# Layer 2 of a mixture-of-experts trunk: the experts' order made behind expert 0, one more expert with a fixed place, and another order of the last expert's work

## The chip, the cores and the metric

One Trainium2 chip, one of its cores. The metric is the device time of one execution in microseconds (us), lower is better. Beside it stands one profiled execution, whose span runs from its first to its last instruction. TensorE (PE in the profile) makes the matrix products; VectorE (DVE), ScalarE (ACT) and GpSimd (POOL) work beside it; SyncE (SP) issues the loads from the chip's memory (HBM).

## The reference, cut to what matters

Two layers on 256 tokens of width 1024. Each has a token mixer (pooling in layer 1, attention in layer 2) and then a mixture of 32 experts, each with a gate, an up and a down matrix of 1024 x 256, 1024 x 256 and 256 x 1024 floats. All arithmetic is float32.

```python
def hier_moe(h, w_group, w_expert, w_gate, w_up, w_down):
    g_prob = jax.nn.softmax((t @ w_group).astype(jnp.float32), axis=-1)
    g_w, g_sel = lax.top_k(g_prob, 1)
    ...
    e_val, e_sel = lax.top_k(e_logits, EXPERT_TOPK)          # top 2 of the 8 in the group
    ...
    for e in range(N_EXPERTS):
        he = jax.nn.silu(t @ w_gate[e]) * (t @ w_up[e])
        y = y + combine[:, e, None] * (he @ w_down[e])
```

Every expert's 3 MB of weights has to come from HBM; an expert sees only the few tokens that chose it.

## The kernel before

**The ring.** Weights come into a ring of four slots, each with room for the gate and up matrices (one load of 2 MB) and the down matrix (one load of 1 MB) of an expert. In what follows GU31 is the load of the gate and up matrices of the expert at place 31, and D31 that of its down matrix. SyncE issues all loads, in program order (the loop at L670): GU(p+1), then D(p), then GU(p+2), D(p+1) and so on to GU31, D30, D31, and last the 0.5 MB of the final norm's gains. A load waits for its slot: GU for `ring_free`, which ScalarE counts up when the gate and up products of the slot's last user are done (L1769), D for `down_free`, counted up after the down product (L1778).

**Places.** In layer 2 the experts 0 to `STAT` - 1 = 6 stand at places of their own number. Experts 4, 5 and 6 have room outside the ring and are loaded early. The other 25 are put in an order that depends on the routing: twelve experts with at most 16 tokens in each half ("light") first, in six pairs (`LIGHTS`), then the rest. The order comes about in three steps. VectorE computes a diagonal matrix (`order_experts`, L2259). TensorE multiplies it by ones (`order_rows`, L1056), which spreads the order over all partitions, in `order_at` of bank 1. VectorE turns that into integers and into lanes for the later compares (`places_by_rows`, L2278), and counts `off_ready` up to 3 and 4, on which SyncE (L667) waits before it reads which expert stands at place 7, and GpSimd before it copies tokens for places from 7 on.

**Units.** `UNITS` (L31) has 26 units, of one place or one light pair, numbered from 0: places 0, 1, 2, 3, the pair (7, 8), place 4, the pair (9, 10), 5, (11, 12), 6, three more pairs, and places 19 to 31. Units 24 and 25 are places 30 and 31. What one unit takes:

- *hidden*: the gate and up products on TensorE (into bank 0 or 1), then a silu on ScalarE and a multiplication on VectorE (`gate_he`);
- *turn*: `turn_he_of`, TensorE transposes the result, VectorE copies it back (`take_heT`);
- *down*: the down product into bank 2 or 3, which VectorE scales into `ye` (`take_ye`);
- *rows*: `rows_unit` adds `ye` to the tokens' rows in banks 4 to 7, by a matrix `share` that VectorE makes (`match_unit`, `share_unit`).

`expert_unit` (L1222) runs on TensorE, for unit u: turn of u-1, hidden of u, down of u-1, and where u is odd rows of u-3 and of u-2. In the last unit (25) it is turn of 24, hidden of 25, down of 24, turn of 25, rows of 22. Then `later_experts` (L1267) runs the down product of unit 25 in two halves of 256 columns, with rows of 23 between them and rows of 24 behind, and `last_rows` adds the last rows half by half. The final norm follows: squares on ScalarE (L2039), the gains, four stores.

**Around expert 0.** On TensorE the gather of the tokens (into hS, part of reg_a in the trace) stands first, then `order_rows`, then the hidden of expert 0 (`first_hidden`, L1066), then `table_light` twice, then turn and hidden of expert 1 (`second_hidden`). GpSimd copies each expert's tokens into xh before its hidden.

Of the kernel before, what the change touches and what calls it, by code (L numbers as in the profile page):

```python
# [7 lines left out]
P = 128  # L8
SEQ, D, F, E = 256, 1024, 256, 32
NG, EPG, TOPK = 4, 8, 2  # L10
NH, DH = 16, 64
T = SEQ // P
# [4 lines left out]
PAD = NSLOT + CAP  # L17
LIGHT = CAP // T
NLP = 6
STAT = 7  # L20
NQ = P // CAP
RANKS = 128
FAR = 65536.0
# [4 lines left out]
FRONT = R + 2  # L28
LOOPED = FRONT + (E - FRONT) // R * R
LIGHTS = [(STAT + 2 * n, STAT + 2 * n + 1) for n in range(NLP)]  # L30
UNITS = [(0,), (1,), (2,), (3,), LIGHTS[0], (4,), LIGHTS[1], (5,), LIGHTS[2], (6,)] + LIGHTS[3:] \  # L31
    + [(p,) for p in range(STAT + 2 * NLP, E)]
NU = len(UNITS)
COUNTED = (E, NU)
# [138 lines left out]
def program(nc, x, c, ada_w, ada_b, norm_mix_g, norm_ffn_g, pool_w, pool_scale, w_qkv, w_o,  # L173
# [3 lines left out]
    with ctx:  # L177
# [50 lines left out]
        pair_first, pair_step = in_alibi(NLP), in_alibi(NLP)  # L228
        light_lanes = in_alibi(T * NLP).rearrange("p (t n) -> p t n", t=T)
        order_f = in_alibi(E)  # L230
        ones = sb("ones", [P, P])
        qkb = sb("qkb", [P, 4])
        ccol = sb("ccol", [P, KC])
# [88 lines left out]
        chosen = ye[0:E, 1, 2 * P:2 * P + E]  # L322
        of_place = ye[0:E, 1, 2 * P + E:2 * P + 4 * E].rearrange("p (f n) -> p f n", f=3)
        order_diag = ye[0:E, 1, 2 * P + 4 * E:2 * P + 7 * E].rearrange("p (f n) -> p f n", f=3)
        of_place_sum = ye[0:E, 1, 2 * P + 7 * E:2 * P + 7 * E + 3]
# [167 lines left out]
        def _(sp):  # L493
# [170 lines left out]
            gate_up(1, 3, *exp_at(1, 3))  # L664
            sp.wait_ge(S("gf_full"), 2)
            up_part(1, early, R)
            sp.wait_ge(S("off_ready"), 3)  # L667
            e = expert_of(STAT)
            gate_up(1, e, *exp_at(1, STAT))
            for p in range(STAT, E):  # L670
                if p + 1 < E:
                    following = expert_of(p + 1)
                    gate_up(1, following, *exp_at(1, p + 1))
                down_part(1, e, *exp_at(1, p))
                e = following
                if p == STAT + 1:
# [156 lines left out]
        def _(pe):  # L833
# [222 lines left out]
            def order_rows():  # L1056

                pe.wait_ge(S("diag_ready"), T + 1)
                pe.wait_ge(S("hS_dve"), 2 * len(BY_DVE))
                mm(order_at, ones[0:E, :], order_diag, True, True).then_inc(S("counts"), 1)  # L1060

            def table_light(t):

# [2 lines left out]
            def first_hidden(L):  # L1066

                s, fill = loaded(L, 0)
                gu = gate_up_w(s).rearrange("p (g k j f) -> p k j g f", g=2, k=KC, j=2)
                pe.wait_ge(S("ring_first", s), fill)  # L1070
                pe.wait_ge(S("ring_mid", s), fill)
                for k in range(KC):
                    pe.wait_ge(S("xe_ready", L), 2 + k // 4)
                    for j in range(2):
                        last = mm(bank[0][j * 64:(j + 1) * 64, 0:F], xe[:, 0, k, :], gu[:, k, j, :, :], k == 0, k == KC - 1)
                last.then_inc(S("gu_ready", L), 1)
                if L == 0:
# [144 lines left out]
            def expert_unit(u):  # L1222

                b = u % 2
                turn_he_of(1, u - 1, 1 - b)
                hidden_unit(u, b)
                down_unit(u - 1, 1 - b, u >= 3)
                if u == NU - 1:
                    turn_he_of(1, u, 1)
                    rows_unit(u - 3, 0)  # L1230
                elif b:
                    rows_unit(u - 3, 0)
                    rows_unit(u - 2, 1)

            def last_rows(L):

# [30 lines left out]
            def later_experts(L):  # L1267

                n = COUNTED[L]
                if L == 0:  # L1270
                    experts(L, FRONT, LOOPED)
                    for e in range(LOOPED, E):
                        expert_at(L, e)
                else:
                    for u in range(2, NU):
                        expert_unit(u)
                n_ovf = beyond(pe, L)
# [367 lines left out]
            mixed_logits(4, 8)  # L1645
            route(1)
            gather(1)
            order_rows()
            for e in range(2):
                expert_at(1, e)  # L1650
            later_experts(1)
# [3 lines left out]
        def _(act):  # L1655
# [411 lines left out]
        def _(dve):  # L2067
# [94 lines left out]
            def route(L):  # L2162
# [82 lines left out]
                if L == 0:  # L2245
                    nc.vector.memset(hS[:, :, NSLOT:PAD], 0.0).then_inc(S("hS_pad"), 1)
                    take_gathered(L)
                else:
                    places_by_rows()

            def take_gathered(L):

# [6 lines left out]
            def order_experts():  # L2259
# [10 lines left out]
                then(nc.vector.tensor_scalar(chosen, place_of[0:E, :], own_part[0:E, :], None, ALU.is_equal))  # L2270
                tt(of_place[:, 0, :], chosen, of_expert[0:E, :], ALU.mult)
                then(tt(of_place[:, 1:3, :], offc[0:E, :].rearrange("p (t n) -> p t n", t=T),
                        chosen.unsqueeze(1).broadcast_to([E, T, E]), ALU.mult))
                then(nc.vector.tensor_reduce(of_place_sum, of_place, AX, ALU.add))
                tt(order_diag, ident[0:E, 0:E].unsqueeze(1).broadcast_to([E, 3, E]),
                   of_place_sum.unsqueeze(2).broadcast_to([E, 3, E]), ALU.mult).then_inc(S("diag_ready"), 1)

            def places_by_rows():  # L2278

                dve.wait_ge(S("counts"), 3)  # L2280
                then(nc.vector.tensor_scalar(order_f[0:1, :], order_at[0:1, 0:E], 1.0 / RANKS, None, ALU.mult))
                nc.vector.tensor_copy(order_i[:, :], order_f[0:1, :]).then_inc(S("off_ready"), 1)
                nc.vector.tensor_copy(off_at, order_at[0:1, E:3 * E]).then_inc(S("off_ready"), 1)
                nc.vector.tensor_scalar(lanes, order_at[:, 0:E], of_lane[:, 0:1], None, ALU.add)
                pairs = order_at[:, STAT:STAT + 2 * NLP].rearrange("p (n x) -> p x n", x=2)
                then(nc.vector.tensor_copy(pair_first, pairs[:, 0, :]))
                then(tt(pair_step, pairs[:, 1, :], pair_first, ALU.subtract))
                then(stt(pair_first, pair_step, second, pair_first, ALU.mult, ALU.add))
# [97 lines left out]
            def expert_unit(u):  # L2386

                b = u % 2
                if u:
                    take_heT(1, u - 1, 1 - b)  # L2390
                if u == 1:
                    dve.wait_ge(S("tab_ready"), 2)
                    for g in range(4):
                        rows = slice(32 * g, 32 * g + 32)
# [10 lines left out]
                    share_unit(u - 2, b)  # L2405
                gate_he(1, u, b)
                if u == 0:
                    count_beyond(1)
                if u >= 2 and b == 0:
                    if u > 2:  # L2410
                        dve.wait_ge(S("rows_added", 1), u - 2)
                    take_ye(1, u - 1, 1)

            def expert(L, e, b, ahead_rows=False, next_rows=False):

# [73 lines left out]
            def later_experts(L):  # L2489
# [3 lines left out]
                    for e in range(LOOPED, E):  # L2493
                        expert_at(L, e)
                else:
                    for u in range(NU):
                        expert_unit(u)
                n_ovf = beyond(dve, L)
                take_heT(L, n - 1, 1)
                if L:  # L2500
                    match_unit(n - 2)
                    dve.wait_ge(S("rows_added", L), n - 3)
                take_ye(L, n - 2, 0)
                if L:
                    share_unit(n - 2, 0)
# [248 lines left out]
```

## Time and profile before

| | us |
|---|---|
| median of the runs | 690.08 |
| lowest, highest of 3 runs | 689.83, 690.11 |
| the profiled execution, its own time | 690.19 |
| span of the profiled execution | 688.5 |
| TensorE busy in it | 626.9 (91%) |
| VectorE, ScalarE, GpSimd busy | 251.1, 120.1, 60.5 |
| moved by DMA | 273.32 MB, mean 397 GB/s |

The profile's page gives the busy time of each engine, the span in 40 slices with the clock that TensorE was granted, the moved bytes for each slice, the chain of work that ended last, and the costliest groups of instructions. The trace behind it gives the single instructions with what ended the idle time before them. A float32 product shows as two matmul records with a weight load each.

### The profile page before, as it was taken

The numbers are of one execution on the slowest core, as the hardware profiler recorded it, in microseconds if no ns is written. First come the engines' busy times: TensorE is split into PE (matmuls) and PEld (weight loads), VectorE is DVE, ScalarE is ACT, GpSimd is POOL, SyncE is SP. The second block draws the span as 40 slices with busy tenths as digits, with TensorE's granted clock in tenths as the row PEclk, the third lists the DMA queues.
The fourth block names the chain that finished last, engine by engine and source line by source line (L and its number), as shares of the span: only waits on it lengthen the run. The fifth ranks groups of instructions, "written<-read, shape, count | busy, mean of one in ns | idle before, by whom it ended". The sixth has DMA issues, their size and how long they took to land.

```text
span 688.5 us, 12940 instructions
## 1 busy us (share of the span) xinstructions
PE 626.9 (91%) x4790; PEld 383.7 (56%) x4790; DVE 251.1 (36%) x668; ACT 120.1 (17%) x312; POOL 60.5 (9%) x187
## 2 busy tenths in 40 slices
PE   4889899999899999999999999999999867998885
PEld 1445465554455555556888788886544324454452
DVE  1014433222222223245689495247332302222223
ACT  4013530000000000014244333237100000000003
POOL 7000021101001001100000000001111100001000
PEclk9999999999999999999999999999999979999998
DMA  9999999999999999999997989963999999999992
GB/s 354 417 420 422 428 421 433 430 428 431 433 430 428 430 428 426 423 420 421 418 422 282 413 343 426 422 277 127 390 425 420 427 427 421 425 426 423 425 419 97
DMA packets 27259, 273.32 MB, mean 397 GB/s; under 512 B 3141, under 2 KB 3653, under 8 KB 4937
## 3 DMA queue, kind: packets, MB, share of 16 engines
q1 hardware_dynamic: 27208, 272.65, 94.7%
q8 instruction: 32, 0.52, 0.3%
q14 instruction: 19, 0.15, 0.1%
HBM read 271.59 MB, written 1.05 MB: 396 GB/s over the span
## 4 chain that ended last, share of the span: by engine, by line
PE 80%; DMA 11%; issue 5%; ACT 1%; DVE 1%; SPq 1%; ACTq 0%; POOL 0%; DVEq 0%
PE bank L835 71%; DMA ring<-in_ada_w_dram 9%; PE bank L1043 6%; DMA ring<-in_exp_w_dram 2%; PE bank L1218 1%; PE bank L1526 1%; SPq L510 0%; ACT hx L2039 0%; PE bank L1380 0%; PE bank L1387 0%; DVE ye L2080 0%; ACT reg_b L1845 0%; ACT reg_a L1710 0%; ACTq L177 0%; DVE ye L2077 0%
## 5 line engine op out<-in xcount | busy, mean ns | idle before, releaser
L835 PE MATMUL bank<-ring,xh 128*64 128x256 f32 (+2 forms) x2496 | 306.0, 429 | 34.9 <-issue 33.9
L835 PEld LDWEIGHTS bank<-ring,xh 128*64 128x64 f32 (+1 forms) x2496 | 169.6, 134 | 132.2 <-issue 75.9
L2077 DVE TENSOR_TENSOR reg_c<-reg_c,bank 128x128 f32<-128x128 f32 x58 | 16.7, 288 | 183.0 <-ACT reg_c L1733 96.5
L763 POOL COPY xh<-reg_a 128x256 f32 (+1 forms) x106 | 41.2, 399 | 410.9 <-PE bank L835 287.2
L835 PE MATMUL bank<-reg_b,ring 128*128 128x256 f32 x256 | 57.2, 380 | 0.4 <-ACT reg_b L1890 0.4
L1043 PE MATMUL bank<-ye,reg_b 32*128 32x512 f32 (+1 forms) x432 | 52.8, 599 | 0.0
L835 PEld LDWEIGHTS bank<-reg_b,ring 128*128 128x128 f32 x256 | 48.0, 190 | 7.1 <-issue 0.9
L2077 DVE TENSOR_TENSOR ye<-bank,reg_c 128x512 f32<-128x512 f32 (+1 forms) x60 | 40.2, 670 | 29.5 <-PE bank L835 29.0
L2341 DVE COPY xh<-bank 128x128 f32<-128x128 f32 x58 | 16.6, 285 | 93.0 <-PE bank L835 93.0
L835 PE MATMUL bank<-ring,cact 128*32 128x512 f32 (+1 forms) x320 | 34.0, 535 | 16.5 <-DMA ring<-in_ada_w_dram 16.4
L1733 ACT ACTIVATE reg_c<-bank 128x128 f32<-128x128 f32 x32 | 8.9, 277 | 203.9 <-PE bank L835 203.9
L1770 ACT ACTIVATE reg_c<-bank 128x128 f32<-128x128 f32 x26 | 7.2, 277 | 185.0 <-PE bank L835 185.0
L835 PEld LDWEIGHTS bank<-cst,reg_c 128*64 128x64 f32 (+1 forms) x240 | 15.4, 138 | 39.5 <-issue 38.3
L1043 PEld LDWEIGHTS bank<-ye,reg_b 32*128 32x128 f32 x432 | 19.3, 184 | 31.1 <-issue 31.0
L835 PE MATMUL bank<-reg_a,ring 128*128 128x256 f32 x160 | 35.8, 381 | 0.0
L2080 DVE SCALAR_TENSOR_TENSOR ring<-ring,cact 128x1024 f32<-128x1024 f32 x28 | 34.2, 1279 | 0.3 <-DVE ring L2080 0.3
L835 PEld LDWEIGHTS bank<-reg_a,ring 128*128 128x128 f32 x160 | 30.0, 190 | 5.5 <-ACT reg_a L1657 0.8
L835 PE MATMUL bank<-ring,reg_b 128*128 128x256 f32 x128 | 28.9, 383 | 0.0
L835 PEld LDWEIGHTS bank<-ring,cact 128*32 128x32 f32 x320 | 8.1, 110 | 34.6 <-DMA ring<-in_ada_w_dram 17.3
L835 PEld LDWEIGHTS bank<-ring,reg_b 128*128 128x128 f32 x128 | 23.9, 190 | 4.1 <-issue 1.1
L835 PE MATMUL bank<-cst,reg_c 128*64 128x128 f32 (+1 forms) x240 | 25.3, 285 | 0.6 <-DVE reg_c L2165 0.6
L2080 DVE SCALAR_TENSOR_TENSOR reg_b<-reg_b,cst 128x256 f32<-128x256 f32 x52 | 24.8, 477 | 0.3 <-issue 0.2
(212 smaller groups left out, 457.0 us busy)
## 6 DMA issues: line engine op xcount, KB each, us to landing
ring<-in_exp_w_dram SPq DMA_DIRECT2D x41, 2048.0 KB, 20.3
ring<-in_exp_w_dram SPq DMA_DIRECT2D x20, 3072.0 KB, 16.0
ring<-in_ada_w_dram SPq DMA_DIRECT2D x48, 1024.0 KB, 17.7
ring<-in_exp_w_dram SPq DMA_DIRECT2D x44, 1024.0 KB, 21.0
ring<-in_w_qkv_dram SPq DMA_DIRECT2D x12, 1024.0 KB, 16.3
ring<-in_w_o_dram SPq DMA_DIRECT2D x4, 1024.0 KB, 8.4
gu_spare<-in_exp_w_dram SPq DMA_DIRECT2D x1, 2048.0 KB, 20.3
hx<-in_exp_w_dram SPq DMA_DIRECT2D x2, 1024.0 KB, 19.5
```

The source lines that it names most:

```text
L763: nc.gpsimd.tensor_copy(xe[:, b, k0:k1, t * CAP:(t + 1) * CAP], hS[:, k0:k1, bass.ds(off, CAP)])\
L835: return nc.tensor.matmul(o_, l_, r_, start=start, stop=stop)
L1043: yield nc.tensor.matmul(bank[4 + half + 2 * t][:, c0:c1], share[rows, b, :], ye[rows, b, c0:c1], start=False, stop=stop, skip_group_check ...
L1218: last = nc.tensor.matmul(bank[4 + half + 2 * t][:, :], share_light[rows, b, t, :], ye[rows, b, :], start=False, stop=False, skip_group_ch ...
L1526: last = nc.tensor.transpose(bank[5 + a][:, s * P:(s + 1) * P], sc[m % 2][a][:, s * P:(s + 1) * P], ident)
L1733: nc.scalar.activation(sil[:, b, :], bank[b][:, 0:P], ACT.Silu).then_inc(S("sil_ready", L), 1)
L1770: nc.scalar.activation(sil[:, u % 2, :], bank[u % 2][:, 0:P], ACT.Silu).then_inc(S("sil_ready", 1), 1)
L2077: return nc.vector.tensor_tensor(o_, a_, b_, op)
L2080: return nc.vector.scalar_tensor_tensor(o_, a_, s_, b_, op0, op1)
L2341: nc.vector.tensor_copy(heT[:, b, :], bank[b][:, 2 * P:3 * P]).then_inc(S("heT_ready", L), 1)
```

## The change

Three things are changed.

1. `STAT` goes from 7 to 8. Expert 7 has a fixed place and is a unit of its own, at index 4; the pairs begin at place 8, and 20 to 31 are single. There are still 26 units, and units 24 and 25 are still places 30 and 31. SyncE issues GU7 ahead of its wait for the order; the loop from there on issues the same loads in the same sequence.
2. The order's product on TensorE stands behind the hidden of expert 0, ahead of `table_light`, over 128 partitions where it had 32. VectorE copies `order_at` out (`keep_order`) behind `gate_he` of unit 0, and TensorE waits for that copy (`counts_read` 3) before the hidden of expert 1, which writes to the same bank. `places_by_rows` works from the copy, in unit 1 ahead of the table's copies, and `count_beyond` moves from unit 0 to unit 1.
3. The last unit has a function of its own on TensorE and on VectorE; ScalarE waits for the down product of unit 24 ahead of the silu of unit 25.

```diff
-STAT = 7
+STAT = 8
-UNITS = [(0,), (1,), (2,), (3,), LIGHTS[0], (4,), LIGHTS[1], (5,), LIGHTS[2], (6,)] + LIGHTS[3:] \
+UNITS = [(0,), (1,), (2,), (3,), (7,), LIGHTS[0], (4,), LIGHTS[1], (5,), LIGHTS[2], (6,)] + LIGHTS[3:] \
...
+            e = STAT - 1
+            gate_up(1, e, *exp_at(1, e))
             sp.wait_ge(S("off_ready"), 3)
-            e = expert_of(STAT)
-            gate_up(1, e, *exp_at(1, STAT))
-            for p in range(STAT, E):
+            for p in range(STAT - 1, E):
...
                 pe.wait_ge(S("diag_ready"), T + 1)
-                pe.wait_ge(S("hS_dve"), 2 * len(BY_DVE))
-                mm(order_at, ones[0:E, :], order_diag, True, True).then_inc(S("counts"), 1)
+                mm(order_at, ones[:, :], order_diag, True, True).then_inc(S("counts"), 1)
...
+                    order_rows()
                     pe.wait_ge(S("diag_ready"), 2 * T + 1)
                     table_light(0)
...
+                if L:
+                    pe.wait_ge(S("counts_read"), 3)
...
+            def last_unit():
+
+                u = NU - 1
+                turn_he_of(1, u - 1, 0)
+                rows_unit(u - 3, 0)
+                down_unit(u - 1, 0, True)
+                hidden_unit(u, 1)
+                rows_unit(u - 2, 1)
+                turn_he_of(1, u, 1)
+                rows_unit(u - 1, 0)
...
                 down(bank[3], down_w(s), 1, 0, 256).then_inc(S("dn_ready", L), 1)
-                if L:
-                    add_rows_of(L, n - 3, 1)
                 down(bank[1], down_w(s), 1, 256, 512).then_inc(S("dn_ready", L), 1)
-                add_rows_of(L, n - 2, 0)
+                if L == 0:
+                    add_rows_of(L, n - 2, 0)
...
+                if u == NU - 1:
+                    act.wait_ge(S("dn_ready", 1), u)
                 act.wait_ge(S("gu_ready", 1), u + 1)
...
+            def keep_order():
+
+                dve.wait_ge(S("counts"), 3)
+                nc.vector.tensor_copy(order_kept, order_at).then_inc(S("counts_read"), 1)
+                dve.wait_ge(S("counts_read"), 3)
```

On TensorE around expert 0, before: the 128x96 product from ye is the order's, the 64x256 ones into bank 0 are the hidden of expert 0, those into bank 1 the hidden of expert 1, the 128x512 ones the two tables.

```order
L835 MATMUL bank3<-keep,reg_b 128x256 x2
L835 MATMUL bank1<-ye,ones 128x96
L835 MATMUL bank0<-ring,xh 64x256 x16
L835 MATMUL bank2<-keep,ones 128x512
L835 MATMUL bank3<-keep,ones 128x512
L835 MATMUL bank0<-cst,reg_c 64x128 x2
L835 MATMUL bank1<-ring,xh 64x256 x16
```

And after, the same place:

```order
L836 MATMUL bank3<-keep,reg_b 128x256 x2
L836 MATMUL bank0<-ring,xh 64x256 x16
L836 MATMUL bank1<-ye,ones 128x96
L836 MATMUL bank2<-keep,ones 128x512
L836 MATMUL bank3<-keep,ones 128x512
L836 MATMUL bank0<-cst,reg_c 64x128 x2
L836 MATMUL bank1<-ring,xh 64x256 x16
```

The order's product went past the sixteen products of expert 0; nothing else moved here.

On TensorE at the end, before: cst,reg_c is a turn, 64x256 x16 a hidden, 64x512 x4 a down, 64x256 x4 half of the last down, ye,reg_b 128x512 x4 the rows of one unit. It begins with the turn of unit 24.

```order
L835 MATMUL bank<-cst,reg_c 64x128 x2
L835 MATMUL bank<-ring,xh 64x256 x16
L835 MATMUL bank<-ring,xh 64x512 x4
L835 MATMUL bank<-cst,reg_c 64x128 x2
L1043 MATMUL bank<-ye,reg_b 128x512 x4
L437 TENSOR_LOAD ov_n
L437 ISA x2
L835 MATMUL bank<-ring,xh 64x256 x4
L1043 MATMUL bank<-ye,reg_b 128x512 x4
L835 MATMUL bank<-ring,xh 64x256 x4
L1043 MATMUL bank<-ye,reg_b 128x512 x4
```

After, from the same turn on:

```order
L836 MATMUL bank<-cst,reg_c 64x128 x2
L1044 MATMUL bank<-ye,reg_b 128x512 x4
L836 MATMUL bank<-ring,xh 64x512 x4
L836 MATMUL bank<-ring,xh 64x256 x16
L1044 MATMUL bank<-ye,reg_b 128x512 x4
L836 MATMUL bank<-cst,reg_c 64x128 x2
L1044 MATMUL bank<-ye,reg_b 128x512 x4
L438 TENSOR_LOAD ov_n
L438 ISA x2
L836 MATMUL bank<-ring,xh 64x256 x8
```

Rows of 22 and the down of 24 went ahead of the hidden of 25; rows of 23 and of 24 stand behind it, and the two halves of the last down follow one another with nothing between.

## Rows read from the trace of the kernel before

**Rows 1.** The page: memory traffic in 40 equal slices of the span.
```profile
GB/s 354 417 420 422 428 421 433 430 428 431 433 430 428 430 428 426 423 420 421 418 422 282 413 343 426 422 277 127 390 425 420 427 427 421 425 426 423 425 419 97
```

**Rows 2.** Waits of the load queue: for whom, us in total, times, longest.
```profile
SPq L590 <- DVE off_i L2283: 10.9, 1, 10.9
```

**Rows 3.** Timeline, 475.8 to 482.3: start, us, engine, line, operation, count, idle before.
```profile
475.90 0.43 PE L835 MATMUL bank<-ye,ones 32*128 32x96 f32 x2 [0.16 <-DVE reg_a L2256]
476.00 0.51 POOL L763 COPY xh<-reg_a 128x128 f32 x1 [1.90 <-ACT reg_a L1710]
476.65 3.67 PE L835 MATMUL bank<-ring,xh 128*64 128x256 f32 x32 [0.32 <-POOL xh L763]
...
477.27 0.20 DVE L2283 CAST off_i<-bank 1x64 int32<-1x64 f32 x1
...
480.26 1.98 PE L835 MATMUL bank<-keep,ones 128*128 128x512 f32 x4
480.45 0.28 ACT L1770 ACTIVATE reg_c<-bank 128x128 f32<-128x128 f32 x1 [2.09 <-PE bank L835]
```

**Rows 4.** TensorE's timeline in the routing: two small products with ones, 128x64 each.
```profile
466.54 0.65 PE L835 MATMUL bank<-ye,ones 128*128 128x64 f32 x4
```

**Rows 5.** Timeline of the load queue, 478 to 495: GU7 and GU8 (one row), D7.
```profile
480.62 6.09 SPq L549 DMA_DIRECT2D ring<-in_exp_w_dram  x2
488.01 0.33 SPq L555 DMA_DIRECT2D ring<-in_exp_w_dram  x1
```

**Rows 6.** Two stretches: from:to, us, TensorE busy, its clock, DMA share, GB/s.
```profile
484.00:486.00 2.00, 2.00 (x22) 1.00 1.02 434
486.00:488.00 2.00, 2.00 (x16) 1.00 0.95 320
```

**Rows 7.** DMA issues, median us to landing: GU7 (480.62), GU8 (486.37), GU20 (580.30).
```profile
ring<-in_exp_w_dram SPq DMA_DIRECT2D x1, 2048.0 KB, 7.6
ring<-in_exp_w_dram SPq DMA_DIRECT2D x1, 2048.0 KB, 8.5
ring<-in_exp_w_dram SPq DMA_DIRECT2D x1, 2048.0 KB, 13.4
```

**Rows 8.** Timeline of the load queue, 640 to 655: GU31; D30 and D31.
```profile
643.56 0.34 SPq L549 DMA_DIRECT2D ring<-in_exp_w_dram  x1
645.20 7.81 SPq L555 DMA_DIRECT2D ring<-in_exp_w_dram  x2
```

**Rows 9.** DMA issues, us to landing: GU31 (issued 643.56), then D30 (issued 645.20).
```profile
ring<-in_exp_w_dram SPq DMA_DIRECT2D x1, 2048.0 KB, 25.4
ring<-in_exp_w_dram SPq DMA_DIRECT2D x1, 1024.0 KB, 26.3
```

**Rows 10.** Timeline of all engines, 666.9 to 681.2.
```profile
667.04 0.39 PE L835 MATMUL bank<-cst,reg_c 128*64 128x128 f32 x4
...
669.10 5.39 PE L835 MATMUL bank<-ring,xh 128*64 128x256 f32 x40 [1.67 <-issue]
672.89 0.28 ACT L1770 ACTIVATE reg_c<-bank 128x128 f32<-128x128 f32 x1 [6.99 <-PE bank L835]
...
674.29 0.42 PE L835 MATMUL bank<-cst,reg_c 128*64 128x128 f32 x4
...
674.64 1.14 PE L1043 MATMUL bank<-ye,reg_b 32*128 32x512 f32 x8
...
675.71 1.08 PE L835 MATMUL bank<-ring,xh 128*64 128x256 f32 x8
...
677.79 1.08 PE L835 MATMUL bank<-ring,xh 128*64 128x256 f32 x8
...
678.81 2.00 PE L1043 MATMUL bank<-ye,reg_b 32*128 32x512 f32 x24
678.92 0.42 DVE L2077 TENSOR_TENSOR ye<-bank,reg_c 128x256 f32<-128x256 f32 x1 [0.37 <-PE bank L835]
680.83 0.60 ACT L2039 ACTIVATE hx<-bank 128x512 f32<-128x512 f32 x1 [6.14 <-PE bank L1043]
```

**Rows 11.** Stretches around two idle times of TensorE; columns as in rows 6.
```profile
549.00:557.00 8.00, 0.00 (x0) 0.67 1.02 428
570.00:572.00 2.00, 0.15 (x4) 1.00 0.98 410
572.00:574.00 2.00, 2.00 (x24) 0.56 1.07 455
```

**Rows 12.** TensorE's timeline, 570 to 579: hidden and down of one unit.
```profile
571.85 7.06 PE L835 MATMUL bank<-ring,xh 128*32 128x256 f32 x80 [3.63 <-issue]
```

More of the change, by code:

```diff
@@ L230, in program @@
         order_f = in_alibi(E)
+        order_kept = in_alibi(3 * E)
         ones = sb("ones", [P, P])
@@ L321, in program @@
         spread = ye[:, 1, 2 * P:4 * P].rearrange("p (v q) -> p v q", v=2)
[L322 to L325, printed above, removed]
+        chosen = ye[:, 1, 2 * P:2 * P + E]
+        of_place = ye[:, 1, 2 * P + E:2 * P + 4 * E].rearrange("p (f n) -> p f n", f=3)
+        order_diag = ye[:, 1, 2 * P + 4 * E:2 * P + 7 * E].rearrange("p (f n) -> p f n", f=3)
+        of_place_sum = ye[:, 1, 2 * P + 7 * E:2 * P + 7 * E + 3]
         Ssb = xe[:, 0, :, :].rearrange("p k c -> p (k c)")[:, 0:SEQ]
@@ L675, in _ @@
                 e = following
-                if p == STAT + 1:
+                if p == STAT:
                     sp.wait_ge(S("tab_full"), 2)
@@ L1227, in expert_unit @@
                 down_unit(u - 1, 1 - b, u >= 3)
[L1228 to L1231, printed above, removed]
+                if b:
                     rows_unit(u - 3, 0)
                     rows_unit(u - 2, 1)
+            def last_unit():
[7 more added lines that the diff above has]
+                rows_unit(u - 1, 0)
             def last_rows(L):
@@ L1274, in later_experts @@
                 else:
-                    for u in range(2, NU):
+                    for u in range(2, NU - 1):
                         expert_unit(u)
+                    last_unit()
                 n_ovf = beyond(pe, L)
@@ L1647, in _ @@
             gather(1)
-            order_rows()
             for e in range(2):
@@ L2247, in route @@
                     take_gathered(L)
-                else:
-                    places_by_rows()
             def take_gathered(L):
@@ L2269, in order_experts @@
                 then(tt(place_of[:, free], others, moved, ALU.add))
[L2270 to L2273, printed above, removed]
+                then(nc.vector.tensor_scalar(chosen, place_of, own_part, None, ALU.is_equal))
@@ L2274, in order_experts @@
+                tt(of_place[:, 0, :], chosen, of_expert, ALU.mult)
+                then(tt(of_place[:, 1:3, :], offc.rearrange("p (t n) -> p t n", t=T),
+                        chosen.unsqueeze(1).broadcast_to([P, T, E]), ALU.mult))
                 then(nc.vector.tensor_reduce(of_place_sum, of_place, AX, ALU.add))
-                tt(order_diag, ident[0:E, 0:E].unsqueeze(1).broadcast_to([E, 3, E]),
-                   of_place_sum.unsqueeze(2).broadcast_to([E, 3, E]), ALU.mult).then_inc(S("diag_ready"), 1)
+                tt(order_diag, ident[:, 0:E].unsqueeze(1).broadcast_to([P, 3, E]),
+                   of_place_sum.unsqueeze(2).broadcast_to([P, 3, E]), ALU.mult).then_inc(S("diag_ready"), 1)
@@ L2278, in places_by_rows @@
+            def keep_order():
+                dve.wait_ge(S("counts"), 3)
+                nc.vector.tensor_copy(order_kept, order_at).then_inc(S("counts_read"), 1)
+                dve.wait_ge(S("counts_read"), 3)
             def places_by_rows():
-                dve.wait_ge(S("counts"), 3)
-                then(nc.vector.tensor_scalar(order_f[0:1, :], order_at[0:1, 0:E], 1.0 / RANKS, None, ALU.mult))
+                then(nc.vector.tensor_scalar(order_f[0:1, :], order_kept[0:1, 0:E], 1.0 / RANKS, None, ALU.mult))
@@ L2282, in places_by_rows @@
                 nc.vector.tensor_copy(order_i[:, :], order_f[0:1, :]).then_inc(S("off_ready"), 1)
[L2283 to L2287, printed above, removed]
@@ L2288, in places_by_rows @@
-                then(stt(pair_first, pair_step, second, pair_first, ALU.mult, ALU.add))
+                nc.vector.tensor_copy(off_at, order_kept[0:1, E:3 * E]).then_inc(S("off_ready"), 1)
+                nc.vector.tensor_scalar(lanes, order_kept[:, 0:E], of_lane[:, 0:1], None, ALU.add)
+                pairs = order_kept[:, STAT:STAT + 2 * NLP].rearrange("p (n x) -> p x n", x=2)
+                then(tt(pair_step, pairs[:, 1, :], pairs[:, 0, :], ALU.subtract))
+                then(stt(pair_first, pair_step, second, pairs[:, 0, :], ALU.mult, ALU.add))
@@ L2391, in expert_unit @@
                 if u == 1:
+                    places_by_rows()
                     dve.wait_ge(S("tab_ready"), 2)
@@ L2407, in expert_unit @@
                 if u == 0:
+                    keep_order()
+                if u == 1:
                     count_beyond(1)
@@ L2412, in expert_unit, with last_unit @@
                     take_ye(1, u - 1, 1)
+            def last_unit():
+                u = NU - 1
+                take_heT(1, u - 1, 0)
+                match_unit(u - 2)
+                dve.wait_ge(S("rows_added", 1), u - 3)
+                share_unit(u - 2, 1)
+                match_unit(u - 1)
+                dve.wait_ge(S("rows_added", 1), u - 2)
+                share_unit(u - 1, 0)
+                take_ye(1, u - 1, 0)
+                gate_he(1, u, 1)
             def expert(L, e, b, ahead_rows=False, next_rows=False):
@@ L2495, in later_experts @@
                 else:
-                    for u in range(NU):
+                    for u in range(NU - 1):
                         expert_unit(u)
+                    last_unit()
                 n_ovf = beyond(dve, L)
                 take_heT(L, n - 1, 1)
[L2500 to L2505, printed above, removed]
+                if L == 0:
+                    take_ye(L, n - 2, 0)
+                else:
                     match_unit(n - 1)
```

## The prediction

> **What bounds the kernel now.** I read the page first, then the waits and the timeline of the load queue, then the trace at the two places that the change touches. The traffic by slices [rows 1] is the view to begin with: nearly every slice stands at 420 to 430 GB/s, so the kernel is a stream of weights. The exceptions are slices in the middle (277 and 127 GB/s at 448 to 482 us), where the stream stops, and the last slice. From 484 us on the stream is full to near its end [rows 6]. So the time is made of three parts: when the stream of layer 2's experts starts again, its bytes at some 425 GB/s, which the change leaves alone, and what still has to be done when the last pieces have landed. TensorE is busy for 91% of the span, but in the last third it waits for each second gate and up load; a product moved there counts only if it lies behind the last landing.
>
> Where the stream starts again: SyncE waits for the order [rows 2], and the conversion that ends this wait runs from 477.27 for 0.20 us [rows 3]. GU7 is nevertheless issued only at 480.62 [rows 5], 0.17 us after the silu of expert 0 begins at 480.45 [rows 3]. That silu marks the end of expert 0's gate and up products, which frees slot 0. So the slot comes last, by some 3 us, and not the order.
>
> **The fixed place of expert 7.** GU7 no longer waits for the order, but it still waits for slot 0. Gain: 0. The order is now needed for GU8, whose slot 1 comes free with expert 1's hidden; before, GU8 was issued at 480.62 + 6.09 - 0.33 = 486.38 [rows 5]. The order now comes at: he of unit 0, turn, its copy on VectorE (about 483.3), then two short steps of VectorE, about 483.8, and some 0.6 us of SyncE to read it. That is 2 us ahead of the slot, so nothing. With 26 units still, and one single unit earlier, TensorE's sum of work over the units is the same. In the middle the stream is held by free slots, and its reserve is thinnest where GU20 landed 13.4 us after its issue, against 7.6 for a load of its size into an empty queue [rows 7]: 5.8 us of reserve, and a shift of the pairs by one unit moves the issue times by less. Nothing.
>
> **The order's product.** Before, it ran 475.90 to 476.33, while GpSimd still copied expert 0's tokens (476.00 to 476.51); expert 0 began at 476.65, released by that copy [rows 3]. It lay in idle time and cost nothing, so taking it away from there gives nothing (at the very most the 0.32 us that TensorE waited). Behind expert 0 TensorE has no idle time: the tables start at once, at 480.26 [rows 3]. There it costs its full length: at most the 0.43 us that its row shows, with a drain that now lies beside other work, and about as much as one of two similar products that took 0.65 together, 0.33 each [rows 4]. I take 0.25, between nothing and 0.43. The wait for the copy of the order adds nothing: VectorE is done with he of unit 0 by 481.2 and with a copy of 96 columns by 481.5, when TensorE is still in the tables (to 482.2). What is queued behind this wait on TensorE is expert 1's hidden, and behind it GU8. So GU8 is issued 0.25 later. Does this reach the stream? GU8 was already late: in 486 to 488 the traffic fell to 320 GB/s, from 434 [rows 6], and GU8 took 8.5 us to land, 0.9 more than into an empty queue [rows 7]. So the stream had all but run dry when GU8 came, and a delay goes through nearly in full: 0.2 us, between 0 and 0.43. On VectorE the steps of `places_by_rows` and of the count (8 and 8 small instructions, most of about 0.2 us like the one at 477.27 [rows 3]) now lie in unit 1; queued behind them is the copy of unit 1's turn, which TensorE needs only after the hidden of unit 2, 5 us later, and the load of D6 waits for the count, but stands behind D8. Nothing.
>
> **The last unit.** This is the term that decides. The new order puts the down product of unit 24, which needs D30, ahead of the hidden of unit 25, which needs GU31. GU31 is issued before D30 [rows 8] and landed at 643.56 + 25.4 = 668.96; D30 landed at 645.20 + 26.3 = 671.50 [rows 8, 9]. Before, TensorE began the hidden at 669.10, 0.14 after GU31 landed, after an idle time of 1.67 us [rows 10]. Now:
>
> - turn of 24 to 667.43, rows of 22 in the idle time, to about 668.45;
> - down of 24 not before 671.50 + 0.14 = 671.64. Its length: hidden and down take 669.10 to 674.29 = 5.19, the hidden of it to the silu at 672.89, 3.75, so the down takes 1.44 [rows 10];
> - hidden of 25 from 673.08, where it was 669.10: 3.98 later, to 676.83.
>
> What is saved behind it: before, from the end of the hidden at 672.85 to the first square on ScalarE at 680.83 there were 7.98 us [rows 10]. Now there are rows of 23, 1.07 (674.64 to 675.71, which also covers silu and he); the turn, 0.35 (674.29 to 674.64); rows of 24, 1.07; two halves of the last down, 2 x 1.02 (677.79 to 678.81); and from there a wait that was covered by rows of 24: the second half of ye starts 0.11 after the down's end and takes 0.42 [rows 10], with the passing on some 0.65, then the last four rows. From the start of rows of 24 at 678.81 to the square took 2.02; that row holds 24 records in 2.00 us, of which rows of 24 are the wide half, 0.97, and the first half of the last rows a quarter, 0.48; less these it leaves 0.57. The sum is 1.07 + 0.35 + 1.07 + 2.04 + 0.65 + 0.57 = 5.75, so 2.23 saved. Net 3.98 - 2.23 = 1.75 us later. The last down, wanted from 679.3, finds D31 there: it is queued right behind D30 (issued at 645.20 + 7.81 - 0.33 = 652.7 [rows 8]), and 1 MB at 425 GB/s is 2.5 us, so it lands at about 674. The final norm behind it is as before. ScalarE's new wait for the down of 24 ends at 673.1, before the silu it stands ahead of; it delays nothing.
>
> **Sum.** 690.19 (the profiled execution, span 688.5 and 1.69 around it) + 0.20 + 1.75 = 692.14. That execution is 0.11 above the median of the runs, so the prediction for the median is **692.0**. With the bounds (front 0 to 0.43 and at best -0.32; the tail +-0.4 for the lengths of pieces taken from single rows) it is 691.2 to 692.7.
>
> **Rivals.**
>
> *The clock falls in the new idle time.* TensorE would stand still from 668.45 to 671.64, 3.2 us. In this trace idle times of 1.67 us leave the clock at its full level, 2.4 GHz; an idle time of 8 us took it to half of that (the mean in the stretch is 0.67), and after one of 3.63 us [rows 12], with 0.15 us of work in the 2 us at its end, the clock stood at a mean of 0.56 [rows 11], nearer to the 1.2 GHz level. Hidden and down then took 578.85 - 571.85 = 7.0 us at least, against 5.2. If this happens in the tail it costs 1.7 us more: 693.7. For it: 3.2 is near 3.63. Against it: the turn and the rows stand right ahead of it. What the Trainium skill says, in "TensorE: Matmul & The Clock Gate", Part 1 on the clock gate, is that the array falls to 1.2 GHz after it has been idle and comes back only after sustained work; the trace agrees at 572 us, and by that rule the cost is the same 1.7. Chance 0.15.
>
> *D30 is there in time, and the tail gains.* If D30 were landed with GU31, the down of 24 would start at 669.10, the hidden at 670.54, 1.44 later, and with 2.23 saved the end would come 0.79 earlier: 690.08 + 0.20 - 0.79 = 689.5, not slower. The point from which it decides: D30 no more than 0.8 us behind GU31; at 671.50 against 668.96 it is 2.54 behind, about what 1 MB takes at 425 GB/s (2.5). Both come by one queue, D30 second. The Trainium skill ("DMA: Bandwidth & Descriptors", Queues, rings and completion order) has it that each DMA engine takes its descriptors in the order of the ring; the landings agree, and this speaks against the rival. Since loads come in pieces on 16 engines, and I may misjudge which wait stands where, 0.12.
>
> *The front gains.* If the first products of expert 0 were held by the order's product after all, the stream would start up to 0.32 earlier, and the sum is 691.4. Chance 0.06. *The order was what held GU7*: it would then go out at 477.5, and the stream would start 3 us earlier, some 689; the slot's release stands against it. Chance 0.03.
>
> *The stream runs dry in the middle.* TensorE's idle times move by a unit, and with the clock halved behind them a slot could come free late by more than the 5.8 us of reserve; a us or two, 693. Chance 0.04.
>
> **How the numbers follow.** The forecast as worked out has 0.60. What a measurement of this kernel can tell from no change is 0.2%, 1.4 us, so the line to "slower" runs at 691.5. The forecast's own lower edge (691.2) and the front's gain lie just under it and give "within" about 0.07 beside the 0.12 of the early D30; faster by over 0.2% has 0.04, nearly all from the order that held GU7. Slower has the rest, 0.77. The range for 8 in 10 runs from 690.9, below the forecast's edge and the front's gain, to 693.8, with the clock's fall; left out are the early D30, the GU7 case and what would lie above.
>
> **What would show it.** In the profile after: the order's product right behind expert 0, expert 0 still at about 476.6, and GU7 issued at about 480.6; GU8 at about 486.6; full traffic from there; rows of 22 right behind the turn of 24, then TensorE idle for about 3.2 us until D30 lands near 671.7, the hidden of 25 from about 673.3, the first square near 682.8. The prediction is wrong if the idle time ahead of the down of 24 is under 1.5 us, if GU7 is issued well before 480, or if the tail's pieces lie apart by more than their lengths.

## The result

| | before | after |
|---|---|---|
| median of the runs, us | 690.10 | 693.92 |
| lowest, highest of 4 runs | 689.83, 690.52 | 693.76, 694.92 |
| span of the profiled execution | 688.5 | 692.3 |

The changed kernel is slower: the ratio of its runs to those of before is 1.0058, with a 95% interval of 1.0046 to 1.007. That is 3.8 us, where 1.9 were forecast, and 0.1 us above the range.

**The front.** The first view is the timeline of the changed kernel around expert 0 (start, us, engine, line, operation); it answers to [rows 3].

```profile
476.09 0.51 POOL L764 COPY xh<-reg_a 128x128 f32 x1 [1.89 <-ACT reg_a L1720]
476.74 3.67 PE L836 MATMUL bank<-ring,xh 128*64 128x256 f32 x32 [0.91 <-POOL xh L764]
...
480.34 0.46 PE L836 MATMUL bank<-ye,ones 128*128 128x96 f32 x2
480.54 0.28 ACT L1782 ACTIVATE reg_c<-bank 128x128 f32<-128x128 f32 x1 [2.08 <-PE bank L836]
...
480.64 1.91 PE L836 MATMUL bank<-keep,ones 128*128 128x512 f32 x4
```

Expert 0 begins at 476.74, released by GpSimd's copy as before (476.65); the place that the order's product left is now idle time, 0.91 in place of 0.32. Behind expert 0 the product costs 0.30 us: the tables begin at 480.64, 0.30 behind the product's start. The load queue, as in [rows 5]:

```profile
480.55 6.47 SPq L550 DMA_DIRECT2D ring<-in_exp_w_dram  x2
488.18 0.38 SPq L556 DMA_DIRECT2D ring<-in_exp_w_dram  x1
```

GU7 goes out with the slot, at 480.55 (before 480.62), and GU8 at 480.55 + 6.47 - 0.33 = 486.69, 0.31 later than before. Of this 0.09 is the start of expert 0 itself, which lies between 476.47 and 476.96 in the profiled executions of all kernels here. Counted from that start, GU8 goes out after 9.95 us where it was 9.73, so 0.22 later.

**The tail.** The load queue of the changed kernel at the end, and how long GU31 (issued 643.82) and D30 (issued 645.46) took to land, answering to [rows 8, 9]:

```profile
643.82 0.34 SPq L550 DMA_DIRECT2D ring<-in_exp_w_dram  x1
645.46 7.81 SPq L556 DMA_DIRECT2D ring<-in_exp_w_dram  x2
```

```profile
ring<-in_exp_w_dram SPq DMA_DIRECT2D x1, 2048.0 KB, 25.4
ring<-in_exp_w_dram SPq DMA_DIRECT2D x1, 1024.0 KB, 26.3
```

So GU31 landed at 669.22 and D30 at 671.76, both 0.26 later than before. And the timeline of the end, against [rows 10]:

```profile
667.30 0.39 PE L836 MATMUL bank<-cst,reg_c 128*64 128x128 f32 x4
...
667.62 1.14 PE L1044 MATMUL bank<-ye,reg_b 32*128 32x512 f32 x8
...
671.83 7.08 PE L836 MATMUL bank<-ring,xh 128*64 128x512 f32 x40 [3.06 <-DMA ring<-in_exp_w_dram]
...
678.84 1.14 PE L1044 MATMUL bank<-ye,reg_b 32*128 32x512 f32 x8
679.02 0.28 ACT L1782 ACTIVATE reg_c<-bank 128x128 f32<-128x128 f32 x1 [12.86 <-PE bank L836]
...
684.62 0.60 ACT L2051 ACTIVATE hx<-bank 128x512 f32<-128x512 f32 x1 [3.81 <-PE bank L1044]
```

Behind the rows of unit 22 TensorE stands still for 3.06 us, until D30 lands. The row that follows is the down product of unit 24 and the hidden of unit 25 in one. Before, the same 40 records took 5.19 us to the next instruction; here they take 678.84 - 671.83 = 7.01. The stretches of the changed kernel tell why (from:to, us, TensorE busy, its granted clock, DMA share, GB/s):

```profile
668.00:670.00 2.00, 0.76 (x8) 1.00 0.99 412
670.00:672.00 2.00, 0.17 (x2) 1.00 0.92 379
672.00:674.00 2.00, 2.00 (x8) 0.70 0.47 188
674.00:676.00 2.00, 2.00 (x10) 0.50 0.06 25
676.00:678.00 2.00, 2.00 (x20) 0.95 0.00 0
```

After the idle time the clock falls from 2.4 to 1.2 GHz (0.50 in 674 to 676) and is back at about 676. The first square comes at 684.62, 3.79 later than before. That is the whole difference of the spans (692.3 - 688.5).

The account of these 3.79 us, from the start of the hidden at 669.10 before: the down product starts at 671.83, 2.73 later (0.26 of this is the stream, which came later); it takes 1.44 itself at full clock; the two products together take 7.01 - 5.19 = 1.82 longer, most of it by the halved clock (1.69 and 0.13 for the new order itself, as experiments 3 and 5 show); behind it 684.62 - 678.84 = 5.78 are left, where 7.98 were, 2.20 saved. 2.73 + 1.44 + 1.82 - 2.20 = 3.79.

### The profile page after: what moved, and what is told of

It reads as the page before. It is cut to its first block, busy times and chain, and to the rows that moved or that the text cites. A ratio compares the mean times of both kernels' runs of the same rounds, so it can differ in the third digit from the quotient of the medians.

```text
span 692.3 us, 12936 instructions
## 1 busy us (share of the span) xinstructions
PE 632.3 (91%) x4790; PEld 385.0 (56%) x4790; DVE 251.1 (36%) x668; ACT 120.1 (17%) x312; POOL 60.5 (9%) x187
## 4 chain that ended last, share of the span: by engine, by line
PE 80%; DMA 13%; issue 4%; DVE 1%; ACT 1%; SPq 1%; ACTq 0%; POOL 0%; DVEq 0%
PE bank L836 71%; DMA ring<-in_ada_w_dram 9%; PE bank L1044 6%; DMA ring<-in_exp_w_dram 4%; PE bank L1221 2%; PE bank L1537 1%; SPq L511 0%; ACT hx L2051 0%; PE bank L1391 0%; PE bank L1398 0%; DVE ye L2092 0%; ACT reg_b L1857 0%; DVE ye L2089 0%; ACT reg_a L1720 0%; ACTq L177 0%
## 5 line engine op out<-in xcount | busy, mean ns | idle before, releaser
L836 PE MATMUL bank<-ring,xh 128*64 128x256 f32 (+3 forms) x2496 | 308.3, 432 | 35.3 <-issue 30.5
```

The costliest lines, as they stand in the source:

```text
L836: return nc.tensor.matmul(o_, l_, r_, start=start, stop=stop)
```

## The experiments

The theory to test: the new last unit holds nearly all of the loss, by the wait for D30 and by the clock that this wait costs; the front is a matter of 0.2 to 0.3 us. Rivals: the stream suffers in the middle; the new order of the tail is slow by itself; the excess over the forecast has another cause than the clock. All times are medians, beside runs of the kernel before on the same chip; a comparison with the changed kernel is one with its 693.92 us.

### 1. The front of the change alone

The changed kernel with `last_unit` taken out again on TensorE and VectorE, and ScalarE's wait with it.

```diff
-                    for u in range(2, NU - 1):
+                    for u in range(2, NU):
                         expert_unit(u)
-                    last_unit()
...
```

> The front of the change alone (expert 7 at a fixed place, the order's product behind expert 0), with the last unit as before. Theory A (the new last unit holds nearly all of the loss; the front only puts 0.2 to 0.3 us of TensorE work ahead of expert 1): 690.3 to 690.4 us against 690.1, the two last loads landing 0.2 to 0.3 later. Rival B (the stream of loads suffers in the middle from the shifted pairs): 691 or more, with slices under 400 GB/s between 500 and 660 us.

Measured: 690.38 us against 690.20, ratio 1.0002 (0.9993 to 1.0011): no difference that can be told. In its profile the hidden of unit 25 starts at 669.38, 0.28 later than before:

```profile
669.38 5.39 PE L836 MATMUL bank<-ring,xh 128*64 128x256 f32 x40 [1.69 <-issue]
```

Its slices of memory traffic from 500 to 650 us stand at 420 to 428 GB/s. The rival with a stream that suffers in the middle falls.

### 2. The new last unit alone

The kernel before, with `last_unit`, the closing lines of `later_experts` and ScalarE's wait as in the change.

> The new last unit alone, on the front of before. Theory A: 693.6 us, that is 3.5 to 3.6 over before, of which about 1.75 is the wait of the down product of unit 24 for its load D30 and about 1.8 the halved clock behind that wait. Rival B: under 692.5.

Measured: 693.75 us, ratio 1.0053 (1.0038 to 1.0069), that is 3.55 over before. The end of its wait, and its stretches:

```profile
671.79 6.87 PE L835 MATMUL bank<-ring,xh 128*64 128x512 f32 x40 [3.11 <-DMA ring<-in_exp_w_dram]
```

```profile
670.00:672.00 2.00, 0.21 (x2) 0.85 0.88 363
672.00:674.00 2.00, 2.00 (x6) 0.50 0.50 197
674.00:676.00 2.00, 2.00 (x14) 0.80 0.08 31
```

So the loss sits in the tail, and the clock falls there without the front too. Front (0.2) and tail (3.55) add up to the whole (3.8).

### 3. Three idle products in the wait

`keep_busy(n, b)` runs n products of 448 columns into bank b; nothing reads them.

```diff
                 rows_unit(u - 3, 0)
+                keep_busy(3, 1)
                 down_unit(u - 1, 0, True)
```

> The changed kernel with three idle products (ident times 448 columns, into bank 1, which nothing reads) on TensorE between the rows of unit 22 and the down product of unit 24, where TensorE otherwise stands still for 3.06 us. They take about 0.75 us each and end before D30 lands. Theory A (the idle time costs the clock, and the halved clock costs 1.8 us): the clock stays at its upper level in the hidden of unit 25 and the time is 692.1 us. Rival C (the clock falls for another reason, or the excess over the forecast comes from elsewhere): 693.9, as without them.

Measured: 692.48 us, ratio 1.0033 (1.002 to 1.0047), 1.4 less than the changed kernel. In the profile:

```profile
668.91 2.52 PE L836 MATMUL bank<-cst 128*128 128x448 f32 x6
...
672.09 5.39 PE L836 MATMUL bank<-ring,xh 128*64 128x512 f32 x40 [0.65 <-issue]
...
677.41 1.14 PE L1044 MATMUL bank<-ye,reg_b 32*128 32x512 f32 x8
```

```profile
672.00:674.00 2.00, 1.92 (x10) 1.00 0.53 213
674.00:676.00 2.00, 2.00 (x22) 1.00 0.09 37
```

The clock stays at 1.00 and the 40 records take 677.41 - 672.09 = 5.32 to the next row, 1.69 less than in the changed kernel. Work that computes nothing makes the kernel faster, so the rival that the clock has no part falls. The gain is 1.4 and not 1.69 because the down product starts 0.26 later in this run (672.09, in the changed kernel 671.83). D30 landed 0.22 later; 0.10 of it stood already at the start of expert 0 (476.84 against 476.74), and the rest stays open. From the rows of unit 23 at 677.41 to the first square at 683.19 there are 5.78 us, as in the changed kernel: this stretch ran at full clock in both.

### 4. One idle product

```diff
+                keep_busy(1, 1)
```

> The changed kernel with one idle product (0.75 us) where the earlier experiment had three. TensorE stands still for about 2.3 us in place of 3.06. Idle times of 1.7 us left the clock alone, one of 3.06 halved it. If 2.3 us are still short enough: 692.2 to 692.5 as with three. If not: 693.9.

Measured: 693.15 us, ratio 1.0047 (1.0032 to 1.0063), from four runs in two groups: 692.28 and 692.36, 693.95 and 694.10. The profiled one is of the first group:

```profile
668.58 1.02 PE L836 MATMUL bank<-cst 128*128 128x448 f32 x2
671.75 5.39 PE L836 MATMUL bank<-ring,xh 128*64 128x512 f32 x40 [2.15 <-issue]
```

```profile
672.00:674.00 2.00, 2.00 (x14) 1.00 0.45 182
```

Here the clock stayed up over 2.15 us of idle time. The groups are 1.7 us apart, the price of the halved clock. That the second group is the clock's fall is inferred from the distance, since only one execution has a profile.

### 5. The down product of unit 24 on weights that had landed

```diff
                 for p in UNITS[u]:
-                    s, fill = loaded(1, p)
+                    s, fill = loaded(1, p - (u == NU - 2))
```

> The changed kernel, but the down product of unit 24 reads the matrix of place 29, which landed some 7 us earlier, in place of the one of place 30; so the matrix of place 30 is left unused, and only the wait for D30 is gone. Theory A (the wait for D30 is the price of the new order, and without it the new order saves): the hidden of unit 25 starts at about 669.9 us, 0.8 later than before, the clock does not fall, 2.2 us are saved behind it, 688.8 us. Rival D (the new order is slower by itself, by pieces that lie further apart): over 690.

This kernel leaves out the down matrix of place 30 and so does not compute the layer; it serves for the time alone.

Measured: 689.08 us against 690.20, ratio 0.9984 (0.9975 to 0.9994). The same order of work, without the wait:

```profile
667.57 1.14 PE L1044 MATMUL bank<-ye,reg_b 32*128 32x512 f32 x8
...
668.64 5.39 PE L836 MATMUL bank<-ring,xh 128*64 128x512 f32 x40
...
673.96 1.14 PE L1044 MATMUL bank<-ye,reg_b 32*128 32x512 f32 x8
...
679.74 0.60 ACT L2051 ACTIVATE hx<-bank 128x512 f32<-128x512 f32 x1 [3.79 <-PE bank L1044]
```

The first square is at 679.74, 1.09 earlier than before. So the new order is not slow by itself; with D30 there it would gain 1.1 us. The wait, with the clock that it costs, is the whole price. Between the first squares of this kernel and of the changed one lie 4.88 us: 3.19 by the later start of the down product (668.64 against 671.83) and 1.69 by the clock (673.96 - 668.64 = 5.32 against 7.01).

### 6. D30 issued ahead of GU31

In SyncE's loop the two loads are swapped at the last place but one; the rest is the changed kernel.

```diff
+                if p == E - 2:
+                    down_part(1, e, *exp_at(1, p))
                 if p + 1 < E:
                     following = expert_of(p + 1)
                     gate_up(1, following, *exp_at(1, p + 1))
-                down_part(1, e, *exp_at(1, p))
+                if p != E - 2:
+                    down_part(1, e, *exp_at(1, p))
```

> The changed kernel with one swap on SyncE: D30 is issued ahead of GU31. The same bytes, the same order of work on TensorE. Theory A: D30 lands before 669, the down product of unit 24 runs at once behind the rows, GU31 lands 2.5 us later than before, at about 671.7, the clock stays up, and the first square comes at 671.8 + 3.75 + 5.71 = 681.3: 690.6 us, 3.3 less than the changed kernel. Rival D (the new order is slow by itself): over 692.

Measured: 690.64 us against 690.16, ratio 1.0005 (0.9996 to 1.0014), 3.3 less than the changed kernel.

```profile
667.93 1.14 PE L1047 MATMUL bank<-ye,reg_b 32*128 32x512 f32 x8
669.00 1.94 PE L839 MATMUL bank<-ring,xh 128*64 128x512 f32 x8
672.15 3.67 PE L839 MATMUL bank<-ring,xh 128*64 128x256 f32 x32 [1.22 <-issue]
```

Nothing was changed on TensorE, and the down product runs at once. The hidden now waits for GU31, issued at 646.94:

```profile
ring<-in_exp_w_dram SPq DMA_DIRECT2D x1, 2048.0 KB, 25.1
```

It lands at 672.04, 2.8 us later than in the changed kernel, with 1 MB ahead of it. The hidden starts 3.05 later than before; less the 2.2 saved behind it, that leaves under 1 us, and in the medians 0.5, not clear of no change. The last 3 MB were put in both sequences here, and in each one of the two products waited for the second piece. The idle time of 1.22 us left the clock at 1.00.

### 7. The order's product behind expert 0, without the fixed place

The front of the change with `STAT` at 7: GU7 waits for the order.

> The front of the change with STAT at 7 in place of 8: the order's product stands behind expert 0, but GU7 needs the order. The last unit as before. Theory A (the fixed place of expert 7 gains nothing by itself and pays for the later order): the order comes at about 483.6 us, GU7 goes out at about 484.2 in place of 480.6, up to 1 us of this is made good by the gap ahead of GU8, and the time is 692.8 to 693.8 us. Rival: the stream makes it good, 690.5.

Measured: 693.22 us, ratio 1.0046 (1.0031 to 1.0062), 3.06 over before. GU7 and GU8 in its load queue:

```profile
484.61 2.36 SPq L550 DMA_DIRECT2D ring<-in_exp_w_dram  x2
```

GU7 goes out at 484.61, 4.1 us later than with the fixed place, GU8 at 486.64 as there. The stream makes up 1 us of it. So the order's product behind expert 0 costs some 3 us unless expert 7 has a fixed place.

### 8. The fixed place alone

The kernel before with `STAT` at 8, GU7 ahead of the wait, and the order's product ahead of expert 0.

> The kernel before with STAT at 8 alone: expert 7 at a fixed place, GU7 ahead of the wait for the order, the order's product still ahead of expert 0, the last unit as before. Theory: GU7 is held by its slot in both, issued at about 480.6, and nothing moves: 690.1 to 690.2 us. Rival: the shifted pairs or the earlier issue change the stream, over 690.5 or under 689.8.

Measured: 690.31 us against 690.23, ratio 1.0001 (0.9992 to 1.001). GU7 and GU8 in its load queue:

```profile
480.29 6.25 SPq L549 DMA_DIRECT2D ring<-in_exp_w_dram  x2
```

GU7 is issued at 480.29 and GU8 at 486.21. Counted from the start of expert 0 (476.47) GU7 goes out after 3.82 us, where it took 3.97 before: a load whose expert is known goes 0.15 sooner. GU8 goes after 9.74 (9.73), and the time does not change. The fixed place is worth nothing for the time by itself.

### 9. Rows of unit 22 into the wait for GU31, on the kernel before

```diff
                 turn_he_of(1, u - 1, 1 - b)
+                if u == NU - 1:
+                    rows_unit(u - 3, 0)
                 hidden_unit(u, b)
                 down_unit(u - 1, 1 - b, u >= 3)
                 if u == NU - 1:
                     turn_he_of(1, u, 1)
-                    rows_unit(u - 3, 0)
...
+                if L:
+                    add_rows_of(L, n - 3, 1)
                 down(bank[3], down_w(s), 1, 0, 256).then_inc(S("dn_ready", L), 1)
-                if L:
-                    add_rows_of(L, n - 3, 1)
```

> The kernel before, with two moves on TensorE in the last unit: rows of unit 22 ahead of the hidden of unit 25, into the 1.67 us in which TensorE waits for GU31, and rows of unit 23 ahead of the last down product's first half, so that the two halves stand together with rows of 24 behind them. The down product of unit 24 stays behind the hidden. Theory A (what counts is the work behind the last gate and up load, and what may go ahead of it is only work whose inputs have landed): one set of rows, 1.07 us, leaves that stretch, 689.1 us against 690.1. Rival: the pieces that stand together now leave a wait of their own, 690.1 or more.

Measured: 689.65 us against 690.16, ratio 0.9992 (0.9983 to 1.0001); half of what was expected, and not clear of no change. The trace has the other half:

```profile
674.61 0.42 PE L835 MATMUL bank<-cst,reg_c 128*64 128x128 f32 x4
...
675.51 1.14 PE L1043 MATMUL bank<-ye,reg_b 32*128 32x512 f32 x8 [0.47 <-DVE xh L2342]
```

The added rows of unit 23 were written behind TensorE's wait for the turned copy of unit 25, so they stood idle for 0.47 us and covered nothing. That was my slip.

### 10. The same with the rows of unit 23 ahead of that wait

```diff
                 turn_he_of(1, u - 1, 1 - b)
+                if u == NU - 1:
+                    rows_unit(u - 3, 0)
                 hidden_unit(u, b)
                 down_unit(u - 1, 1 - b, u >= 3)
                 if u == NU - 1:
                     turn_he_of(1, u, 1)
-                    rows_unit(u - 3, 0)
+                    rows_unit(u - 2, 1)
...
                 down(bank[3], down_w(s), 1, 0, 256).then_inc(S("dn_ready", L), 1)
-                if L:
-                    add_rows_of(L, n - 3, 1)
```

> As the earlier kernel with rows of unit 22 ahead of the hidden of unit 25, but rows of unit 23 stand ahead of TensorE's wait for the turned copy of unit 25, where that kernel had put them behind it: its trace shows 0.47 us of idle time between the turn and those rows. Theory: the rows cover the copy, the 0.47 go, and the time is 689.2 us against 690.1 to 690.2. Rival: the 0.47 come back further on (the halves of ye), 689.6.

Measured: 688.86 us against 690.23, ratio 0.9981 (0.9972 to 0.999).

```profile
667.21 1.14 PE L1043 MATMUL bank<-ye,reg_b 32*128 32x512 f32 x8
...
668.95 5.39 PE L835 MATMUL bank<-ring,xh 128*64 128x256 f32 x40 [0.61 <-issue]
...
674.15 0.42 PE L835 MATMUL bank<-cst,reg_c 128*64 128x128 f32 x4
...
674.49 1.14 PE L1043 MATMUL bank<-ye,reg_b 32*128 32x512 f32 x8
...
675.56 1.95 PE L835 MATMUL bank<-ring,xh 128*64 128x256 f32 x16
...
677.44 2.00 PE L1043 MATMUL bank<-ye,reg_b 32*128 32x512 f32 x24
...
679.46 0.60 ACT L2039 ACTIVATE hx<-bank 128x512 f32<-128x512 f32 x1 [4.92 <-PE bank L1043]
```

The hidden starts as before (668.95), 0.61 us of idle time are left ahead of it, and from there to the first square it is 10.51 us, where it was 11.73 [rows 10]. This kernel beats both. Its two halves of the last down also stand together, as in the change. It does what the change's tail does with the rows of unit 22, and leaves the product whose weights come last but one behind the one whose weights have come.

## Why the prediction was right and where it was wrong

**What bounds it: right.** The stream restarts with the slot and not with the order: GU7 at 480.62 with the wait for the order, at 480.55 and 480.29 without it. Experiment 7 shows the order deciding: there GU7 waits for it, to 484.61. In that run the last of the order's conversions on VectorE ends at 483.65, so SyncE took about 1.0 us to read it, where the prediction allowed 0.6; in the changed kernel GU8's slot comes 2 us behind the order, and the difference has no effect.

**The front, 0.20: right, too small to be told in the time.** The order's product costs 0.30 where it stands now (0.25 taken) and frees nothing where it stood. From the start of expert 0 it moves GU8 by 0.22; the medians of experiment 1 differ by 0.18.

**The wait for D30: right.** Idle 3.06 us (3.2 forecast), the down product at 671.83 (671.64), 2.54 between the landings as before. The part saved behind the last hidden was put at 5.75 us left; it is 5.78. The forecast for a profiled execution, 692.14 without the clock, is where the kernel stands when the clock is held up: 692.48 with three idle products, 692.3 in the first group of experiment 4.

**The clock: wrong.** This is the step that failed: the sum set what the idle time costs the clock at nothing. The mechanism stood among the rivals, with 1.7 us (1.69 measured) and a time of 693.7, but with a chance of 0.15. I gave the turn and the rows right ahead of the idle time as a reason against it, and called 3.2 merely near the 3.63 that had cost the clock. Layer 2 of the trace of before had idle times of 1.67 to 2.17 without a fall and of 3.63 and 8.58 with one, and the 3.2 of the forecast lay closer to the second. What the runs put in its place: the clock fell in both profiled executions with such a wait (3.06 and 3.11), and all four times of each kernel lie within 693.65 to 694.92, none at the 692 of a kept clock. With 2.15 us it seems to fall in some runs and not in others. The rule that I cited from the Trainium skill ("TensorE: Matmul & The Clock Gate", Part 1), that an idle array goes to 1.2 GHz, agrees with the two traces of the longer wait (0.50 behind it); behind 1.67 and the profiled 2.15 the clock stood at 1.00. I weighed the rule too low.

The rival's 1.7 was in part luck. The 7.0 us that it took for the halved clock are those of a pair of light experts, and it set them against the 5.2 of a single unit. A pair at full clock takes 3.59 and 1.86 us for the same products (528.41 to 532.00 and 537.54 to 539.40 in the trace of before), 5.45 together, so this pair lost 1.55 us.

**The order of the two products: 0.13 left out.** At full clock the down product ahead of the hidden takes 5.32 us to the next row, in experiments 3 and 5, where the hidden ahead of the down took 5.19. The next row is the rows of a unit there and a turn here, and part of the 0.13 may lie in that. The sum took the lengths over unchanged.

**The range.** Its upper end, 693.8, was the rival's own figure with 0.1 added, where the bounds of the other terms would have added 0.6 (0.23 for the front, 0.43 less 0.20, and 0.4 for the tail). An end that rests on a rival needs that rival's spread too. The forecast's own bounds, 691.2 to 692.7, are 0.1 above what its terms give from 692.0 (691.1 to 692.6).

**The rivals on the other side.** An early D30 would have gained 0.6 by my sum, the front's loss included; experiment 5 shows 1.1 in the median, with a down product that starts 0.46 sooner than I had set it. The front's gain, the order that held GU7, and a stream that runs dry in the middle did not show: between 500 and 660 us the changed kernel's traffic is 419 to 427 GB/s. TensorE's two long idle times there did change, from 8.58 and 3.63 us to 5.87 and 6.24, with the clock at 0.50 behind both, and the stream did not suffer.

## What to carry to other kernels

At the end of a stream of loads, order the consumers in the sequence in which their data land, and fill the wait for the last large piece only with work whose inputs are already there. Price an idle time of TensorE twice, once as time and once as what the clock costs the products behind it. When a step that produces an address or an order is moved later, find the first load that needs it and put something independent in between.

## What the runs showed of the hardware

Idle products that write to an unread bank were worth 1.4 us here: they hold the clock at 2.4 GHz over a wait for a load. The fall of the clock after a given idle time is not the same in each run: in the profiled executions, in layer 2, it did not show with 1.67 or with 2.17 us and showed with 3.06, 3.11, 3.63, 5.87, 6.24 and 8.58. With 2.15 the times of four runs split into two groups 1.7 us apart; of the eight runs with 3.06 or 3.11 two have a profile, and the times of the other six lie with them. What decides between the groups stays open. The fall costs 1.69 us over products that take 5.32 at 2.4 GHz (7.01 against 5.32). At the very start of the span the profile's clock can't be read so: behind the first wait of 8.56 us it shows 1.00 in the kernel before, but eight products (128x512) took 1.93 us there that take 1.06 at 13.46 us. Whether the clock was low there is not shown.
